# RWKV's 64x64 products placed over all four quadrants of TensorE, in a two-layer hybrid encoder kernel

## The reference

```python
def step(S, inp):
    r_t, w_t, k_t, v_t, kk_t, a_t = inp
    sa = jnp.einsum('bhvk,bhk->bhv', S, -kk_t)
    S = (S * w_t[:, :, None, :] + sa[..., None] * (kk_t * a_t)[:, :, None, :]
         + v_t[..., None] * k_t[:, :, None, :])
    return S, jnp.einsum('bhvk,bhk->bhv', S, r_t)
```

## Time and profile before

| | |
|---|---|
| median of three runs | 3390.58 us |
| the profiled execution | 3393.81 us, span 3391.7 us |
| TensorE matmul busy | 3313.9 us (98%) |
| TensorE weight load busy | 2793.0 us (82%) |
| VectorE busy | 1353.0 us (40%) |
| ScalarE busy | 871.8 us (26%) |
| mean DMA rate | 128 GB/s |

### The profile page before, as it was taken

The page is one execution under the profiler, slowest core; times in us unless marked ns, Lnnn a source line. Parts: engine busy times, 40 slices in busy tenths (PEclk is TensorE's granted clock), DMA queues, the critical chain, the costliest instruction groups (busy, mean ns, idle before and its releaser), DMA issues.

```text
span 3391.7 us, 51457 instructions
## 1 busy us (share of the span) xinstructions
PE 3313.9 (98%) x21652; PEld 2793.0 (82%) x21652; DVE 1353.0 (40%) x3195; ACT 871.8 (26%) x2576; POOL 34.0 (1%) x47
## 2 busy tenths in 40 slices
PE   8989999999999999999999999999999999998997
PEld 6768888888888888878888888888888888887886
DVE  4335452344514444163541534415443244423432
ACT  3223340223403232032420423204231133311211
POOL 0000000000000000000000000000000000000000
PEclk9999999999999999999999999999999999999998
DMA  6134234442344324443334432444334443343442
GB/s 200 51 104 132 90 116 143 143 137 94 125 154 146 127 92 145 151 131 125 100 119 152 137 115 95 143 143 137 112 113 155 155 133 98 129 151 118 160 151 93
DMA packets 128724, 433.76 MB, mean 128 GB/s; under 512 B 13280, under 2 KB 25696, under 8 KB 128368
## 3 DMA queue, kind: packets, MB, share of 16 engines
q1 hardware_dynamic: 127344, 426.28, 38.8%
q0 software_dynamic: 1152, 4.19, 0.3%
HBM read 426.22 MB, written 4.19 MB: 127 GB/s over the span
## 4 chain that ended last, share of the span: by engine, by line
PE 95%; DVE 2%; ACT 1%; issue 1%; DMA 0%; SPq 0%; POOL 0%; DVEq 0%; POOLq 0%; ACTq 0%
PE psum L805 64%; PE psum L1237 18%; PE psum L799 2%; PE psum L819 2%; PE psum L1044 1%; PE psum L1058 1%; PE psum L1056 1%; PE psum L1003 1%; PE psum L1185 1%; PE psum L1074 1%; PE psum L1167 0%; PE psum L1137 0%; PE psum L929 0%; ACT hT L516 0%; PE psum L1140 0%
## 5 line engine op out<-in xcount | busy, mean ns | idle before, releaser
L805 PE MATMUL psum<-hT,slots 128*128 128x256 f32 (+1 forms) x8832 | 2012.0, 386 | 15.8 <-ACT hT L516 7.3
L805 PEld LDWEIGHTS psum<-hT,slots 128*128 128x128 f32 x8832 | 1662.2, 191 | 298.4 <-issue 36.6
L1237 PE MATMUL psum<-gT,slots 128*128 128x256 f32 (+1 forms) x2816 | 618.5, 382 | 0.0
L1237 PEld LDWEIGHTS psum<-gT,slots 128*128 128x128 f32 x2816 | 535.0, 190 | 82.1
L1316 DVE SCALAR_TENSOR_TENSOR hT<-hT,psum 128x256 f32<-128x256 f32 (+1 forms) x128 | 54.4, 425 | 655.5 <-PE psum L1237 548.7
L742 ACT ACTIVATE last<-psum 128x2 f32<-128x2 f32 x352 | 60.2, 171 | 912.5 <-PE psum L805 912.5
L507 ACT ACTIVATE scr<-hT 128x256 f32<-128x256 f32 (+1 forms) x128 | 50.6, 420 | 707.0 <-DVE hT L1334 681.6
L805 PE MATMUL psum<-mixT,slots 128*128 128x256 f32 (+1 forms) x1024 | 229.1, 383 | 2.4 <-DVE hT L1316 1.8
L805 PEld LDWEIGHTS psum<-mixT,slots 128*128 128x128 f32 x1024 | 193.4, 190 | 36.8 <-issue 7.7
L1775 DVE TENSOR_SCALAR tmpG<-raw,par 128x256 f32<-128x256 f32 (+1 forms) x176 | 63.0, 358 | 394.8 <-ACT raw L743 394.8
L1775 DVE TENSOR_SCALAR gT<-raw,par 128x256 f32<-128x256 f32 (+1 forms) x176 | 62.4, 355 | 353.5 <-ACT raw L743 353.3
(11 more groups left out here) (238 smaller groups left out, 2572.6 us busy)
## 6 DMA issues: line engine op xcount, KB each, us to landing
slots<-in_weights SPq DMA_DIRECT2D x792, 512.0 KB, 3.4
hT<-in_x SPq DMA_DIRECT2D x8, 512.0 KB, 5.3
out<-prpt POOLq DMA_DIRECT2D x8, 512.0 KB, 3.0
tab<-in_tables SPq DMA_DIRECT2D x6, 512.0 KB, 4.9
con<-in_consts SPq DMA_DIRECT2D x1, 1562.0 KB, 10.6
tab<-in_tables SPq DMA_DIRECT2D x2, 544.0 KB, 5.1
par<-in_params SPq DMA_DIRECT2D x2, 386.5 KB, 5.3
con<-in_consts SPq DMA_DIRECT2D x1, 66.5 KB, 2.0
```

The costliest lines, as they stand in the source:

```text
L805: ins = mm(psum[:, i % 2, :n], lhsT, rhs, start=k == 0, stop=k == len(pairs) - 1)
L1237: ins = mm(psum[:, i % 2, :n], w[:, e * P:(e + 1) * P], gT[:, k, :n], start=k == 0, stop=k == KF - 1)
```

## The change

It reorders and moves 64x64 products; it adds none and drops none.

- `tile_out`: heads outer, chunks inner, and the products of lines 931 and 932 grouped by pair of heads, so that four consecutive products use four quadrants.
- `scores` and `pairs`: the loop over the head's parity moves inside, next to the chunk's.
- Levels, for groups of two tiles: the second stage's results go to two banks, line 1056's to R0 and line 1058's to R1. Line 1058 writes chunk 0's block to the high half and chunk 1's to the low half (`there`), except in the last level, which puts them back. `Y1` of levels 1 to 4 is exchanged likewise. So in levels 0 to 3 line 1056 and line 1058 use different pairs of quadrants.
- ScalarE's copy of `TT` reads R0 and R1 with another pattern: 64 elements from one bank, 64 from the other.

```diff
--- before.py
+++ after.py
@@ -629,7 +629,7 @@
                         a.wait_ge(S["w_tt"], lev + l + 1)
                         m0 = 1 if l == levels_of(j0) - 1 else 0
                         act(TT.rearrange("p i h m s -> p (i h) m s")[:n, :4 * ng, m0:, :w],
-                            psum[:n, R0:R0 + ng, :].rearrange("p i (h m s) -> p (i h) m s", h=4, m=2)[:, :, m0:, :w],
+                            psum[:n, R0 + m0:R0 + 2, 0:256 * ng].rearrange("p m (h s) -> p h m s", s=HD)[:, :, :, :w],
                             ACT.Copy).then_inc(S["w_ttc"], 1)
                         if l == 0:
                             a.wait_ge(S["w_lkv"], g_ + 1)
@@ -919,17 +919,23 @@
                 if nth:
                     pe.wait_ge(S["w_znew"], znew_before(nth))
                     pe.wait_ge(S["w_yc"], nth)
-                for cc, w, cs in chunks_in(n):
-                    for h in range(4):
-                        ct, hh, pb = h // 2, h % 2, HD * (h % 2)
-                        Bt = BK[cs, i, ct, 0, hh * HD:(hh + 1) * HD]
-                        Kt = BK[cs, i, ct, 1, hh * HD:(hh + 1) * HD]
-                        o, b = ct * HD, bank(R0 + cc)
-                        if j:
-                            mm(b[pb:pb + HD, o:o + HD], X[cs, i, h, 0:HD], Bt, start=True, stop=True)
-                        o += P
-                        mm(b[pb:pb + HD, o:o + HD], Kt, Vt[i][cs, h * HD:(h + 1) * HD], start=True, stop=False)
-                        mm(b[pb:pb + HD, o:o + HD], Bt, X[cs, i, h, HD:], start=False, stop=True)
+                for h in range(4) if j else ():
+                    ct, pb = h // 2, HD * (h % 2)
+                    for cc, w, cs in chunks_in(n):
+                        mm(bank(R0 + cc)[pb:pb + HD, ct * HD:(ct + 1) * HD], X[cs, i, h, 0:HD], BK[cs, i, ct, 0, pb:pb + HD],
+                           start=True, stop=True)
+                for ct in range(2):
+                    o = P + ct * HD
+                    for h in (2 * ct, 2 * ct + 1):
+                        pb = HD * (h % 2)
+                        for cc, w, cs in chunks_in(n):
+                            mm(bank(R0 + cc)[pb:pb + HD, o:o + HD], BK[cs, i, ct, 1, pb:pb + HD], Vt[i][cs, h * HD:(h + 1) * HD],
+                               start=True, stop=False)
+                    for h in (2 * ct, 2 * ct + 1):
+                        pb = HD * (h % 2)
+                        for cc, w, cs in chunks_in(n):
+                            mm(bank(R0 + cc)[pb:pb + HD, o:o + HD], BK[cs, i, ct, 0, pb:pb + HD], X[cs, i, h, HD:],
+                               start=False, stop=True)
                 if j:
                     for h in range(4):
                         ct, pb = h // 2, HD * (h % 2)
@@ -993,44 +999,47 @@
                     ins.then_inc(S["w_tr"], 1)
                     yield
 
-                    def scores(tag, b, col, hh, off):
-
-                        pb = HD * hh
-                        dst = bank(b)[:, col:col + 256].rearrange("p (t m s) -> p t m s", t=2, m=2)
+                    def scores(tag, b, col, off):
+
                         for ct in range(2):
-                            for cc, w, cs in chunks_in(n):
-                                a0 = 2 + off + HD * cc
-                                ins = mm(dst[cs, ct, :, :w], rows[pb:pb + HD, ROW[f"{tag}{ct}"], a0:a0 + w],
-                                         rows[pb:pb + HD, first + ct:first + ct + 7:6, a0:a0 + w], start=True, stop=True)
+                            for hh in range(2):
+                                for cc, w, cs in chunks_in(n):
+                                    a0, pb = 2 + off + HD * cc, HD * hh
+                                    dst = bank(b + hh)[:, col:col + 256].rearrange("p (t m s) -> p t m s", t=2, m=2)
+                                    ins = mm(dst[cs, ct, :, :w], rows[pb:pb + HD, ROW[f"{tag}{ct}"], a0:a0 + w],
+                                             rows[pb:pb + HD, first + ct:first + ct + 7:6, a0:a0 + w], start=True, stop=True)
                         return ins
 
-                    def pairs(b, hh, off):
-
-                        pb = HD * hh
+                    def pairs(b, off):
+
                         for ct in range(2):
-                            for cc, w, cs in chunks_in(n):
-                                a0 = 2 + off + HD * cc
-                                ins = mm(bank(b)[cs, 256 + ct * HD:256 + ct * HD + w], rows[pb:pb + HD, ROW[f"q{ct}"], a0:a0 + w],
-                                         rows[pb:pb + HD, ROW[f"b{ct}"], a0:a0 + w], start=True, stop=True)
+                            for hh in range(2):
+                                for cc, w, cs in chunks_in(n):
+                                    a0, pb = 2 + off + HD * cc, HD * hh
+                                    ins = mm(bank(b + hh)[cs, 256 + ct * HD:256 + ct * HD + w],
+                                             rows[pb:pb + HD, ROW[f"q{ct}"], a0:a0 + w],
+                                             rows[pb:pb + HD, ROW[f"b{ct}"], a0:a0 + w], start=True, stop=True)
                         return ins
                     pe.wait_ge(S["w_trc"], 2 * g_ + 2)
                     for i, (j, off, _) in enumerate(group):
-                        for hh in range(2):
-                            scores("b", R0 + 2 * i + hh, 0, hh, off)
-                            ins = pairs(R0 + 2 * i + hh, hh, off)
+                        scores("b", R0 + 2 * i, 0, off)
+                        ins = pairs(R0 + 2 * i, off)
                     ins.then_inc(S["w_s1"], 1)
                     yield
                     if u:
                         yield
                     pe.wait_ge(S["w_t0"], nth + 1)
                     for i, (j, off, _) in enumerate(group):
-                        for hh in range(2):
-                            ins = scores("k", R0 + hh, 256 * i, hh, off)
+                        ins = scores("k", R0, 256 * i, off)
                     ins.then_inc(S["w_s2"], 1)
                     yield
                     if gi == 0:
                         pe.wait_ge(S["smallV"], SMALL_FREED[u, "pk1"])
                     pe.wait_ge(S["w_t0"], nth + ng)
+
+                    def there(l, cs):
+
+                        return slice(HD - cs.start, 2 * HD - cs.start) if ng == 2 and 0 < l < levels else cs
                     for l in range(levels):
                         last = l == levels - 1
                         if l == 0:
@@ -1041,7 +1050,7 @@
                             for h in range(4):
                                 for cc, w, cs in chunks_in(n):
                                     a0 = 256 * i + h * HD
-                                    ins = mm(bank(R2)[cs, a0:a0 + w], S1[cs, i, h, 1, :w], TT[cs, i, h, 0, :w],
+                                    ins = mm(bank(R2)[there(l, cs), a0:a0 + w], S1[cs, i, h, 1, :w], TT[cs, i, h, 0, :w],
                                              start=True, stop=True)
                         ins.then_inc(S["w_y1"], 1)
                         yield
@@ -1049,13 +1058,16 @@
                         if l == 0:
                             pe.wait_ge(S["w_mask2"], g_ + 1)
                         for i in range(ng):
-                            dst = bank(R0 + i).rearrange("p (h m s) -> p h m s", h=4, m=2)
                             for h in range(4):
+                                a0 = 256 * i + h * HD
                                 if not last:
                                     for cc, w, cs in chunks_in(n):
-                                        mm(dst[cs, h, 0, :w], TT[cs, i, h, 1, :w], Y1[cs, i, h, :w], start=True, stop=True)
+                                        at = there(l, cs)
+                                        mm(bank(R0)[cs, a0:a0 + w], TT[at, i, h, 1, :w], Y1[at, i, h, :w], start=True, stop=True)
                                 for cc, w, cs in chunks_in(n):
-                                    ins = mm(dst[cs, h, 1, :w], Y1[cs, i, h, :w], TT[cs, i, h, 1, :w], start=True, stop=True)
+                                    at = there(l, cs)
+                                    ins = mm(bank(R1)[there(l + 1, cs), a0:a0 + w], Y1[at, i, h, :w], TT[at, i, h, 1, :w],
+                                             start=True, stop=True)
                         ins.then_inc(S["w_tt"], 1)
                         if l == 0:
                             for i in range(ng):
```

## The result

The changed kernel takes 3343.9 us (median of four runs, 3343.58 to 3343.92) where the kernel before takes 3390.7 us. The ratio is 0.9856, with a 95% interval of 0.9843 to 0.9868: 46.8 us less. The forecast was 3340.5 us.

A forecast was written before the change was run, and what follows sets the result against it. TensorE's stream was taken to bound the kernel. Savings of 29.8 + 13.7 + 6.7 + 0.5 + 0.3 = 51.0 us, less 1 us for waits, net 50, took the median of 3390.6 to 3340.5 us; range 3334 to 3364.

The forecast's parts named there:

- The bound: Whole kernel: TensorE has matmul records in flight for 98% of the span, so time taken from its stream shortens the run.
- The pace of four quadrants: RWKV stages: each of four live quadrants keeps about 58 ns per record; stage length is busiest quadrant's records x pace + 0.146 us.
- a sum of 51.0: RWKV stages: savings of 29.8 (second stages), 13.7 (`tile_out`), 6.7 and 0.5 (scores), 0.3 us (meta groups).
- the meta groups: Two groups with 16-wide blocks and few records: orders improve a little, 0.3 us saved, between 0 and 1 us.
- The order: `tile_out`: runs of at most two records per quadrant suffice, being below the eight `scores("k")` is seen to pass over.
- The charge of 1 us: First full tile: TensorE waits 0.86 us longer for VectorE's state update behind a reciprocal; 1 us charged, bounds 0 and 3.
- The remark that two runs differ by 0.02%: Whole runs: two runs of this kernel differ by about 0.02%; 0.2% (6.8 us) bounds what can be told from no change.
- A: Four-quadrant stages: record starts are limited as a whole, 22 ns midway; 28 us saved, 3362 us; chance 12%.
- B: RWKV stretches: gain given back in waits as ScalarE or VectorE falls behind; 3366 us if half is lost; chance 6%.
- C: Four quadrants take turns when two write one bank or half, each stepping every 117 ns; time stays 3390 us; chance 4%.
- D: Levels: crossed and straight pairs exclude each other, each change costing a 0.146 us restart; slower, 3445 us; chance 4%.

The follow-up runs named there:

- the second one of before: Profile of the kernel before, unedited, run once more; ten runs gave 3390.76 to 3395.65 us, median 3393.81 us.
- the yardstick run: The whole change, unedited, on another chip than the first four runs, against the kernel before: 3342.8 us against 3393.9, ratio 0.9851.
- the levels' run: Only the levels' part of the change (second-stage results in two banks, line 1069's on exchanged halves), against the kernel before: 3362.7 us against 3393.1, ratio 0.9911.
- the run of four: The changed kernel with runs of four records per quadrant in the second stages (two heads of one line, then of the other): 3343.1 us.
- the run of eight: The changed kernel with runs of eight records per quadrant in the second stages, per tile one line then the other: 3354.0 us against before's 3393.9, ratio 0.9883.

## Why the prediction was right

**The bound.** TensorE's stream set the time. The profile of the changed kernel and the second one of before differ by 48.5 us in span (3390.1 - 3341.6), those of the yardstick run by 50.3; busy time of the other engines changed by 2.4 us at most, and no wait on them grew by more than 0.1 us but one.

**The pace of four quadrants.** It holds for a whole stage: second stages take 1.09 us, one hundredth over the 1.08 forecast, because the crossed pair starts 13 ns after the straight one. The level 0 stage has 2.01 us as forecast, `tile_out` 2.03 (2.01), first scores 1.50 (1.49), second scores 1.04 (1.02). Added up over the trace, from each stage's first record to the next stage's first, the RWKV stages take 245.2 us in the second profile of before and 194.3 us in the yardstick's: 50.9 us less, against a sum of 51.0. Of the 50.9 us, 0.4 are no work of the change: before, a stage of lines 961 and 966 lay in the stretch at half clock at 161.5 us. By terms the same count gives 29.5 us for the second stages (forecast 29.8), 13.6 for `tile_out` (13.7), 7.0 for the scores (7.2) and 0.3 for the meta groups (0.3). In whole runs, the runs of one part each gave 30.4, 12.2 and 6.9 us where the terms were 29.8, 13.7 less 0.9, and 7.2.

**The order.** The prediction took placement and order together. The runs part them: with the change's placement and runs of sixteen, four fifths of the gain of a second stage in levels 1 to 3 are gone. The sentence that runs of at most two are short enough was right; the reason given, that `scores("k")` passes over eight, was loose. What counts is the run on one quadrant, four there, and at most three records can wait. The prediction had no such rule; that its order has runs of two was a safe choice made on a loose reason.

**What is late next.** The charge of 1 us was right in size: 1.0 us, in the run with `tile_out` alone and in the whole change. Its cause was right in part: VectorE was indeed held by other work when the stage ended. The place was wrong. TensorE waits in front of an earlier product of line 967, for VectorE's line 1587, and not longer for the state update behind the reciprocal; that wait stayed at 2.9 us.

**The difference of 3.4 us** between 3340.5 and 3343.9 is not a step of the argument. The saving was put at 50 us; the first comparison shows 46.8, the second 51.1, the parts sum to 49.5. Runs of the kernel before lie between 3390.3 and 3395.7 us, and the forecast subtracted from the median of three at its low end; had it started from 3393.9 us, as in the second comparison, it would have said 3343.9 us, where that comparison measured 3342.8. The remark that two runs differ by 0.02% came from those three and was too narrow; 0.15% is nearer.

**The rivals.** A needed starts slower than 15.5 ns over 64 records; they come 15.0 ns apart on average, the slower opening of the stage included. The Trainium skill's floor of about 25 ns from start to start ("TensorE: Matmul & The Clock Gate", under "Wait — 56ns, not 53.3ns?") does not hold across quadrants: the trace disagrees, 64 records in 1.09 us. B did not happen: in the levels' run no wait for ScalarE or VectorE grew by more than 0.2 us, and in the changed kernel ScalarE's copy kept its median of 1.02 us. C and D are excluded by the same stage. A restart like the one that D feared does exist, with 0.05 us over the 0.04 that D called decisive, but it is not paid at the changes between the two lines, because with runs of two no quadrant runs out of records. How much of that is owed to the two banks stays open: a version with exchanged halves but one bank for both results would have two quadrants of different input halves write the same bank and the same output half, and it was not tried.

## What to carry to other kernels

Count the records on each quadrant of a stage of 64x64 products: the busiest one times its pace (58 ns for 64 float32 columns, 109 ns for 128), plus 0.15 us for entering and leaving the stage, gave the length of every stage of full tiles above within 0.02 us, as long as the order rotates over the quadrants. Where a chain of products keeps its data on its own half, writing an intermediate to the other half moves half the work to idle quadrants; here that cost nothing but 13 ns per stage. A stage that must stay on two quadrants can take in independent work for the other two. Keep runs on one quadrant to two records. In all stages here quadrants of the same output half wrote to different banks; whether that is needed was not tried. And judge an edit of 0.2% by stage lengths in the profile, since whole runs scatter by 0.15%.

## What the runs showed of the hardware that was not expected

- Records start out of program order across quadrants, but only so far: instructions leave in order, each quadrant holds three records that wait, and a fourth blocks all quadrants behind it (five of eight had started when the next quadrant's first did, and one of four in the run of four). Runs of 2, 4, 8 and 16 records on a quadrant made the same 64 records take 1.09, 1.14, 1.49 and 1.84 us.
- A quadrant that ran dry lost about 50 ns when it started again (0.11 us to its second record in place of 0.06), and in the run of four one step was 35 ns longer without a rule for it.
- The Trainium skill says that a weight load overlaps running matmuls only when their row groups differ ("TensorE: Matmul & The Clock Gate", Part 3, in its list of what overlaps). In the earlier trace rows the record of line 931 at 864.82 is on L->L and runs 0.22 us; the weights of line 929's record at 864.83, on L->H with the same input half, load within that time, so the trace disagrees (the end of a matmul record is modelled, its start is not):

```profile
864.83 0.19 PEld L929 LDWEIGHTS psum<-wset 64*64 64x64 f32 x2
```

- Behind the 2.9 us wait at 161.6 us the clock granted to TensorE was at half in the profile shown of before and full in the one after, where the same wait lies at 159.0 us: 1.05 against 0.61 us for the same 16 records. It does not go with the change: in the run of eight, a changed kernel too, the same stage takes 1.05 us at a granted clock of 0.50.
